# Splitting the weights' low part into two GpSimd instructions of 128x1024, each with its own increment

## What is computed

```
def swiglu(h, w_gate, w_up, w_down):
    return einsum(silu(h @ w_gate) * (h @ w_up), w_down)

# first block, per layer
x = x + mixer(rmsnorm(x, norm_mix[i]))
x = x + swiglu(rmsnorm(x, norm_ffn[i]), w_gate, w_up, w_down)

# second block, per layer
z = rms_norm(x, ln_mix_pre[l]) @ w_in[l]
merged = sum(gates[m] * (branch[m] @ w_branch[l, m]) for m in range(4))
x = x + rms_norm(merged @ w_mix_out[l], ln_mix_post[l])
x = x + rms_norm(cross_attention(rms_norm(x, ln_xa_pre[l]), rms_norm(mem, ln_mem[l])), ln_xa_post[l])
x = x + rms_norm(square(relu(rms_norm(x, ln_mlp_pre[l]) @ mlp_w1[l])) @ mlp_w2[l], ln_mlp_post[l])
```

## Time and profile before

| | |
|---|---|
| time, median of 3 runs | 4382.73 us (4376.33 to 4385.43) |
| profiled execution | span 4367.8 us from its first to its last instruction; its own device time isn't listed |
| TensorE busy | 3840.5 us, 88% |
| VectorE, ScalarE, GpSimd busy | 1824.4, 1209.0, 1263.9 us (42%, 28%, 29%) |
| mean granted clock of TensorE | 0.890 of full speed |
| DMA | 292.42 MB, mean 67 GB/s |

### The profile page before, as it was taken

How to read it: one execution, slowest core, us unless ns; L and a number is a source line. 1 busy time by engine, 2 the same in 40 slices (tenths; PEclk the granted TensorE clock), 3 DMA queues, 4 the chain that set the end, 5 groups by cost and what they waited for, 6 DMA issues and landing times.

```text
span 4367.8 us, 49579 instructions
## 1 busy us (share of the span) xinstructions
PE 3840.5 (88%) x17197; PEld 2982.5 (68%) x17197; DVE 1824.4 (42%) x2706; ACT 1209.0 (28%) x1673; POOL 1263.9 (29%) x279
## 2 busy tenths in 40 slices
PE   5999998989997895887998899979678799898997
PEld 4788775557885653665877678858356587776886
DVE  4421424444125224664445461431456534636252
ACT  2332312333322211223333322221122333333221
POOL 2344531013543320002434134424000043422442
PEclk8999997569998985888999999989568799999998
DMA  2333320002332310001323123322000032312332
GB/s 97 96 87 105 87 87 29 0 28 80 95 94 71 107 59 1 1 1 49 106 87 116 39 87 97 96 76 89 2 1 1 16 108 89 105 59 68 97 96 67
DMA packets 384374, 292.42 MB, mean 67 GB/s; under 512 B 17737, under 2 KB 379683, under 8 KB 383688
## 3 DMA queue, kind: packets, MB, share of 16 engines
q1 hardware_dynamic: 375304, 285.67, 21.3%
q10 hardware_dynamic: 8896, 4.46, 0.4%
HBM read 286.92 MB, written 3.16 MB: 66 GB/s over the span
## 4 chain that ended last, share of the span: by engine, by line
PE 75%; DVE 10%; issue 7%; POOL 4%; ACT 3%; DMA 1%; DVEq 0%; SPq 0%; ACTq 0%; POOLq 0%
PE ps L453 19%; PE ps L457 18%; PE ps L456 18%; POOL w_lo L439 4%; PE ps L903 3%; PE ps L885 3%; PE ps L892 2%; PE ps L1326 1%; DVE y_f L1871 1%; PE ps L1320 1%; PE ps L1545 1%; PE ps L1536 1%; DVE acc L492 1%; PE ps L1543 1%; PE ps L1408 1%
## 5 line engine op out<-in xcount | busy, mean ns | idle before, releaser
L439 POOL TENSOR_TENSOR w_lo<-w_raw,w_hi 128x2048 fp32r<-128x2048 f32 x274 | 1263.5, 4611 | 3054.8 <-ACT w_hi L433 3054.8
L453 PE MATMUL ps<-h_hi,w_hi 128*128 128x512 f32 x2752 | 1088.3, 395 | 80.3 <-POOL w_lo L439 32.1
L456 PE MATMUL ps<-h_lo,w_hi 128*128 128x512 f32 x2752 | 1080.4, 393 | 0.0
L457 PE MATMUL ps<-h_hi,w_lo 128*128 128x512 f32 x2752 | 1079.7, 392 | 0.0
L433 ACT ACTIVATE w_hi<-w_raw 128x2048 fp32r<-128x2048 f32 x274 | 523.4, 1910 | 747.1 <-PE ps L453 683.9
L453 PEld LDWEIGHTS ps<-h_hi,w_hi 128*128 128x128 f32 x2752 | 521.5, 190 | 201.5 <-issue 51.1
L456 PEld LDWEIGHTS ps<-h_lo,w_hi 128*128 128x128 f32 x2752 | 521.8, 190 | 112.6 <-issue 2.1
L457 PEld LDWEIGHTS ps<-h_hi,w_lo 128*128 128x128 f32 x2752 | 520.7, 189 | 112.0
L453 PE MATMUL ps<-hid_hi,w_hi 128*128 128x512 f32 x864 | 338.4, 392 | 7.5 <-POOL w_lo L439 6.9
L456 PE MATMUL ps<-hid_lo,w_hi 128*128 128x512 f32 x864 | 336.3, 389 | 0.0
L457 PE MATMUL ps<-hid_hi,w_lo 128*128 128x512 f32 x864 | 336.3, 389 | 0.0
(11 more groups left out here) (364 smaller groups left out, 4850.7 us busy)
## 6 DMA issues: line engine op xcount, KB each, us to landing
w_raw<-mlp_w SPq DMA_DIRECT2D x128, 512.0 KB, 4.5
w_raw<-w_in SPq DMA_DIRECT2D x112, 512.0 KB, 4.5
w_raw<-ffn_w_gate SPq DMA_DIRECT2D x44, 512.0 KB, 4.0
w_raw<-ffn_w_up SPq DMA_DIRECT2D x44, 512.0 KB, 5.2
w_raw<-xa_wkv SPq DMA_DIRECT2D x32, 512.0 KB, 4.0
w_raw<-ffn_w_down SPq DMA_DIRECT2D x32, 384.0 KB, 3.8
w_raw<-attn_w_qkv SPq DMA_DIRECT2D x24, 512.0 KB, 4.1
w_raw<-ffn_w_down SPq DMA_DIRECT2D x32, 320.0 KB, 3.5
```

The lines of the kernel that those rows point to most:

```text
L439: pool.tensor_tensor(w_lo[:, slot], w_raw[:, slot], w_hi[:, slot].bitcast(F32), ALU.subtract)\
L453: ins = pe.matmul(o, whi[:, kw, cols], rhi(kr), start=a == 0, stop=False)
L456: pe.matmul(o, whi[:, kw, cols], rlo(kr), start=False, stop=False)
L457: ins = pe.matmul(o, wlo[:, kw, cols], rhi(kr), start=False, stop=a == n - 1)
```

## The change

`split_lo` issues two instructions of 128x1024 in place of one of 128x2048, and each increments `w_split`, so a chunk is now worth 2. TensorE waits for the first increment where it waited before. For the second it waits ahead of the first matmul group that reads the second 1024 columns: at contraction tile 4 of the first output tile where a chunk is 8 by 256, at tile 8 of a down projection, at the up product of `gate_and_up`, at the second contraction tile of a branch chunk. Chunks of no more than 1024 columns (4 of the 274) skip it. The loads of SP wait for both halves of chunk k in place of TensorE's beginning of it.

```diff
-    for who, value in (("sp", -2), ("act", -1), ("pool", -1)):
+    for who, value in (("act", -1), ("pool", -1)):
         start(chunk_begun, who, value)
+    start(w_split, "sp", -4)
...
     def load(slot, *parts):
-        wait(sp, take(chunk_begun, "sp"))
+        wait(sp, take(w_split, "sp", 2))
...
         pool.wait_ge(*take(hi_done, "pool"))
         wait(pool, take(chunk_begun, "pool"))
-        pool.tensor_tensor(w_lo[:, slot], w_raw[:, slot], w_hi[:, slot].bitcast(F32), ALU.subtract)\
-            .then_inc(w_split, 1)
+        for a in range(2):
+            half = slice(1024 * a, 1024 * a + 1024)
+            pool.tensor_tensor(w_lo[:, slot, half], w_raw[:, slot, half], w_hi[:, slot, half].bitcast(F32), ALU.subtract)\
+                .then_inc(w_split, 1)
...
-    def product(o, w, cols, rhs, kts, begin=False, arrive=None):
+    def product(o, w, cols, rhs, kts, begin=False, arrive=None, second=None):
...
-        n = len(kts)
+        n, late = len(kts), max(kw for kw, _ in kts) + 1 if second is None else second
         for a, (kw, kr) in enumerate(kts):
+            if begin and second is not None and kw == late:
+                pe.wait_ge(*take(w_split, "pe"))
...
         w = parts_of(slot, kt, c)
+        if kt * c <= 1024:
+            skip(w_split, "pe", 1)
...
-                    arrive=arrive if t == 0 else None)\
+                    arrive=arrive if t == 0 else None, second=1024 // c if kt * c > 1024 else None)\
...
             pe.wait_ge(*take(up_scaled, "pe"))
+            pe.wait_ge(*take(w_split, "pe"))
             product(ps[:, 2 * c + 1, :], parts_of(c, DT, P, 1024), whole, hm, kts).then_inc(tile_done, 1)
...
-                        arrive=None if c else hid_ready).then_inc(tile_done, 1)
+                        second=8, arrive=None if c else hid_ready).then_inc(tile_done, 1)
...
         for a in range(DT):
+            if begin and a == DT // 2:
+                pe.wait_ge(*take(w_split, "pe"))
             ins = pe.matmul(o, rhi(a)[:, tok], whi[:, a, :], start=a == 0, stop=False)
```

More of the change, by code:

```diff
@@ L597, in pool_pe @@
                 pe.wait_ge(*take(bank_free, "pe"))
+                if (g % 2, t) == (1, 0):
+                    skip(w_split, "pe", 1)
                 product(ps[:, (2 * g + t) % 4, :], parts_of(g // 2, 4, 256), slice(P * t, P * t + P), hm,
```

## The result

| | before | after |
|---|---|---|
| median of the runs | 4379.53 us (4370.94 to 4385.43, 4 runs) | 4325.42 us (4311.10 to 4334.11, 4 runs) |
| profiled span | 4367.8 us | 4332.3 us |
| mean granted clock, profiled | 0.890 | 0.889 |

The ratio of the times is 0.988, 95% interval 0.986 to 0.991: about 52 us less, with the interval's ends at 40 and 64. The forecast was 4322 us, by a gain of 61 us on the profiled execution. Run again beside other kernels, the changed kernel gave 4325.32 us, 0.989 [0.987, 0.992] of the kernel before, whose 19 runs there had a median of 4369.93 us: 47 us less.

A forecast was written before the change was run, and what follows sets the result against it. TensorE, busy 88% of the span, was taken to bound the kernel, with 72.1 us of waits for `w_lo` as prize. Terms of 64 us less 3 gave 61: span 4307, plus 14.9, 4322 us; range 4305 to 4350.

The forecast's parts named there:

- term 1: Second down projection, both feed-forwards: split loop falls from 7.29 to TensorE's 6.8 us a chunk, first wait goes; 10 us.
- term 2: Second chunk of a stage, seven places: each wait 2.25 us shorter, 15.7 us, and half clock behind them regained, 14 us.
- term 3: Single short waits, all shorter than 2.3 us, vanish with 0.1 us of slow restart each; 8 us.
- term 4: Memory stage, twice: DVE's tiles set the first five chunks, then the split loop speeds up; 6 us a layer, 12 us.
- term 5: Five places where a blocked DVE instruction gets its turn between the halves, saving 0.6 to 0.85 us each; 4 us.
- costs: Second GpSimd instructions, added TensorE waits, second halves pushed back by DVE, and load timing; 3 us off the sum.
- clock isn't regained: Rival: second chunks' waits shorten but the half clock stays, so term 2 loses its 14 us: 4336 us; chance 0.14.
- GpSimd keeps the port: Rival: GpSimd doesn't let go between halves, or DVE's turns push second halves into TensorE's way: 4336 us; chance 0.12.
- (a): Fixed part of a second GpSimd instruction, taken as 0.1 us; half of it on some 25 remaining waits, 1.2 us.
- (c): Second parts pushed back by DVE's turn, 3.0 against 2.7 us, in the 8 by 256 chunks that waited; 1.5 us.
- The waits inside the chunks: 270 added TensorE waits cost nothing where already met; slower rival 0.2 to 0.4 us each, 4430 us at 0.4; chance 0.05.
- change hands: Rival: ACT's split or the load comes late by what was won, so TensorE waits as long: 4368 us; chance 0.06.

The follow-up runs named there:

- later loads: Changed kernel, but a load also waits for TensorE's first matmul of the slot's last chunk, as before the change: 4321.94 us, 0.990 of the kernel before.
- The early copy: Kernel before, with ScalarE's copy for a stage's second chunk issued ahead of the norm's square root: 4348.89 us, 0.996; on the changed kernel 4298.15 us, 0.983.
- the waits alone: Kernel before, one 128x2048 instruction counting by two, with TensorE's added mid-chunk waits already met: 4382.10 us, 1.0018 of the kernel before.
- four parts and the early copy: Changed kernel with four 128x512 instructions and ScalarE's second-chunk copy ahead of the norm's square root: 4286.88 us, 0.982 of the kernel before.
- eight parts: Changed kernel with the low part in eight instructions of 128x256, TensorE waiting for each where first used: 4312.08 us, 0.987 of the kernel before.
- four parts: Changed kernel with four instructions of 128x512, TensorE waiting for each where first used: 4300.30 us, 0.985; again 4308.58 us, 0.987 of the kernel before.

## Why the prediction was right

By its steps, with the chunks of the profile after:

| | forecast | measured |
|---|---|---|
| term 1, second down projection | 10 | 10.3 |
| term 2, idle and clock | 15.7 + 14 | 13.2 + 11.2, and 0.6 in the chunks ahead |
| term 3, short waits | 8 | 7.9 |
| term 4, memory stage | 12 | 10.4 |
| term 5, DVE between the halves | 4 | 4.3 |
| costs | -3 | in the rows above |
| sum | 61 | 57.9, before the next row |
| cross attention, at half clock | none | -6.2 |

Small differences at other places take back another 2.0 us, so chunks and rest make 49.7. The mixers' 14 us come and go with the execution (with later loads they are -8), so I don't count them as the change's.

**The number 4322** is closer than the forecast deserves. It adds 14.9 us to the span, as the distance between the profiled execution and the median. In every profiled run that has both on record the time is 1.7 to 1.8 us above the span (4334.11 and 4332.3), so the profiled execution of before took some 4369.6 us, and the three-run median of 4382.73 was high; 19 later runs have 4369.93. The gain was forecast as 61 us and is 47 to 54 by the times and 50 by the chunks. That the sum lands 3 us from 4325 is the high start making up for the high gain, so in part luck. The places and the ways of the gain are not.

**Term 1** came out step by step: 6.8 us from start to start, no wait at the first.

**Term 2** has its mechanism right. The early copy shows it: with ScalarE's copy out of the queue all seven waits go. In size it was a sixth too high. Two of the seven waits are only 0.6 to 0.7 us shorter (4.32 became 3.69, and 2.96 became 2.29), since the chunk ahead of each ended 1.4 to 1.5 us sooner and the copy did not start earlier by as much: their share of the gain lies one chunk ahead. The other five are 1.7 to 3.7 us shorter. The clock came back behind five, not six, and not where I had put the exception: the wait of 5.44 us shrank to 1.74 and kept its clock, behind that of 3.69 half of the loss came back, behind that of 2.29 none (the chunk takes 12.4 us before and after). Among these seven it stayed up behind 2.1 us and less. But that is no rule: in the second trace of the same kernel the clock stayed up behind a wait of 2.16 us and fell behind one of 1.85. The forecast's boundary by the length of the wait was a guess that came out five times in seven. The rival "clock isn't regained" is out, though it happened in full once and by half once.

**Term 4** fell out at 5.2 us a layer for 6. DVE's tiles set the pace of the first chunks, as said, and the wait of 0.98 us inside the chunk takes back what the earlier start gives.

**Term 5** rests on DVE getting a turn between the halves. It does: 2.50 against 4.66 us. The rival in which GpSimd keeps the port is out. But the turn is also a price. Of DVE's instructions 105 were stretched before, by 305 us in all against the shortest of their kind; after, 137 are, by 203 us.

**The costs** I sized too low. (a) 0.1 us for a second instruction: by the durations it is 0.19, and by the starts of a pair 0.15. (c) DVE's turn pushes the second half back by 0.4 us, nearly everywhere in the tight stretches, not only in a few chunks. The cut by itself costs 20 us, not 3. It did the sum little harm, because that price falls on the end of the second half, and TensorE only asks for it 2.7 or 5.4 us into the chunk; with the first half put to use TensorE stands at a second half in the memory stage alone. This is a cost that is hidden, and the hiding was in the forecast's own count of 12 and 24 matmuls.

**The waits inside the chunks** cost nothing at their place, as the earlier trace rows had it (of the 8 us that the waits alone brought, a part stays unexplained), and **the loads** showed no cost and no gain. The waits didn't change hands.

**What was missing** is the clock elsewhere. In the cross attention the first of its output chunks has 3.4 us of half clock after the change and none before; together with the stretch ahead of it 3.1 us in each layer. It comes and goes: the kernel with two instructions and no use of them has it in both layers, the one with four parts and the early copy not in the first, and no edit touches the place. Why the clock falls there stays open.

One sign was off: TensorE's waits for the low part went to 43 us, not to some 30. In the memory stage five chunks a layer still wait twice, and their first waits are shorter without being gone.

## What to carry to other kernels

When a consumer waits for a producer's large instruction, cut the instruction and count what the consumer does before it needs each piece; if that is longer than a piece, the price of the cut is hidden, as most of it was here. Before moving work into an engine's idle time, look at whom the engine that it releases will hold up. And when one trace is compared with another, sum the difference by stage first: here two stretches that no edit touches differed by up to 24 us together from one trace to the next.

## What the runs showed of the hardware

- A GpSimd subtraction of 128xN in 32 bits took 185 ns and 2.16 ns a column, from 256 to 2048 columns (737, 1292, 2397, 4606 ns).
- DVE and GpSimd took turns by the instruction when both had work: with one piece or two, eight DVE instructions were stretched by 4.3 us, with four pieces by 2.1 us, where the last one or two of the eight met the split.
- A table load of ScalarE takes 1.28 us each time, and one stood ahead of a plain copy behind a square root, in the place where TensorE was waiting for that copy.
- The mixers' stretch, without a change in its instructions, took between 408.5 us (two instructions, no use of the first) and 429.9 us (eight parts), with DVE's busy time equal to 0.1 us and TensorE's granted clock between 0.74 and 0.68. Between the two traces of four parts it makes 10 of the 13 us of difference.
